# Stream 2 of a two-block transformer layer: the products of the residue groups read their moving operand in residue order

## The reference, cut to what matters

```python
ATT_GROUPS = ((128, 1), (512, 4), (2048, 16))
h = rms_norm_2(x, norm1_w)
proj = h @ w_in                      # q_b, k_b, v_b: 3 x 1536 columns of it
q_b = rms_norm_2(heads(q_b), attn_q_norm_w)
k_b = rms_norm_2(heads(k_b), attn_k_norm_w)
v_b = heads(v_b)
for gi, (window, dil) in enumerate(ATT_GROUPS):
    o_g, l_g = dilated_window_attention(q_b[:, :, gi], k_b[:, :, gi], v_b[:, :, gi],
                                        slopes[gi], dil, window // (2 * dil))
wts = jax.nn.softmax(jnp.stack(lses), axis=0)
o_b = jnp.einsum('gbsh,gbshe->bshe', wts, jnp.stack(outs))
```

## Time and profile before

| | |
|---|---|
| median of 3 runs | 3162.69 us (3160.27 to 3166.07) |
| the profiled execution's own time | 3160.64 us |
| its span in the trace | 3158.8 us |
| granted TensorE clock, mean over the span | 0.96 of 2.4 GHz |
| busy: TensorE, VectorE, ScalarE, GpSimd | 94%, 67%, 50%, 9% of the span |

### The profile page before, as it was taken

How to read it: one execution, slowest core, us unless ns; L and a number is a source line. 1 busy time by engine, 2 the same in 40 slices (tenths; PEclk the granted TensorE clock), 3 DMA queues, 4 the chain that set the end, 5 groups by cost and what they waited for, 6 DMA issues and landing times. The chain is left out here.

```text
span 3158.8 us, 46233 instructions
## 1 busy us (share of the span) xinstructions
PE 2976.5 (94%) x18534; PEld 2388.9 (76%) x18534; DVE 2114.9 (67%) x2176; ACT 1591.3 (50%) x1767; POOL 278.9 (9%) x225
## 2 busy tenths in 40 slices
PE   5999999789999999999999958997999999899999
PEld 4777787468888787788878746887778887778877
DVE  6567654569998998999899964566353344356642
ACT  3556433357777777777777733223454442333321
POOL 0110010001111111111111000442000000000000
PEclk9999999789999999999999979999999988999999
DMA  6322343369999999999999952001211122323321
GB/s 247 123 90 84 105 152 109 123 246 373 371 373 371 376 374 372 368 366 375 374 374 368 364 186 67 3 4 40 72 61 61 57 69 67 112 75 93 95 92 67
DMA packets 217372, 607.95 MB, mean 192 GB/s; under 512 B 10784, under 2 KB 118304, under 8 KB 183424
## 3 DMA queue, kind: packets, MB, share of 16 engines
q1 hardware_dynamic: 202480, 554.87, 47.6%
q0 software_dynamic: 14592, 50.36, 4.6%
q10 hardware_dynamic: 144, 0.53, 0.0%
HBM read 582.62 MB, written 23.10 MB: 192 GB/s over the span
## 5 line engine op out<-in xcount | busy, mean ns | idle before, releaser
L2475 DVE TENSOR_TENSOR weight_ring_part<-weight_ring,weight_ring_part 128x2048 fp32r<-128x2048 f32 x380 | 852.8, 2285 | 105.6 <-ACT weight_ring_part L2414 105.1
L2414 ACT ACTIVATE weight_ring_part<-weight_ring 128x2048 fp32r<-128x2048 f32 x380 | 714.3, 1915 | 257.3 <-PE ps L193 137.0
L193 PE MATMUL ps<-weight_ring_part 128*128 128x512 f32 x1456 | 584.8, 402 | 0.0
L293 DVE TENSOR_TENSOR weight_ring_part<-weight_ring,weight_ring_part 128x2048 fp32r<-128x2048 f32 x111 | 253.2, 2281 | 238.9 <-ACT weight_ring_part L290 236.4
L189 PE MATMUL ps<-weight_ring_part,gathered_hi 128*128 128x512 f32 x1024 | 409.4, 400 | 0.0
L193 PE MATMUL ps<-weight_ring_part,gathered_hi 128*128 128x512 f32 x1024 | 405.7, 396 | 0.0
L192 PE MATMUL ps<-weight_ring_part,gathered_lo 128*128 128x512 f32 x1024 | 405.6, 396 | 0.0
L189 PE MATMUL ps<-h1T_hi,weight_ring_part 128*128 128x512 f32 x872 | 363.3, 417 | 3.1 <-DVE weight_ring_part L293 1.7
L192 PE MATMUL ps<-h1T_hi,weight_ring_part 128*128 128x512 f32 x872 | 351.4, 403 | 0.0
L193 PEld LDWEIGHTS ps<-weight_ring_part 128*128 128x128 f32 x1456 | 280.2, 192 | 70.2
L290 ACT ACTIVATE weight_ring_part<-weight_ring 128x2048 fp32r<-128x2048 f32 x111 | 211.1, 1901 | 133.2 <-PE ps L193 103.9
(11 more groups left out here) (491 smaller groups left out, 4445.1 us busy)
## 6 DMA issues: line engine op xcount, KB each, us to landing
weight_ring<-in_w SPq DMA_DIRECT2D x190, 2048.0 KB, 8.7
weight_ring<-in_w_in SPq DMA_DIRECT2D x58, 1024.0 KB, 5.2
weight_ring<-in_w_ffn_up SPq DMA_DIRECT2D x44, 512.0 KB, 4.8
weight_ring<-in_w_ffn_down SPq DMA_DIRECT2D x11, 1024.0 KB, 4.8
mod_tile<-in_w_ada POOLq DMA_DIRECT2D x36, 256.0 KB, 3.0
weight_ring<-in_w_ada SPq DMA_DIRECT2D x8, 1024.0 KB, 12.8
gate_rows<-in_w_ada POOLq DMA_DIRECT2D x28, 256.0 KB, 3.2
weight_ring<-in_w_branch SPq DMA_DIRECT2D x6, 1024.0 KB, 5.5
```

Of the source, the lines that this page charges most:

```text
L193: return nc.tensor.matmul(out, x[0], y[1], start=False, stop=stop)
L293: self.nc.vector.tensor_tensor(lo, full, hi, ALU.subtract).then_inc(self.split, 1)
L2414: nc.scalar.activation(hi_half(h), full_half(h), ACT.Copy).then_inc(w_rounded, 1)
L2475: nc.vector.tensor_tensor(lo_half(h), full_half(h), hi_half(h), ALU.subtract).then_inc(w_split, 1)
```

## The change

The products of the elements of groups 1 and 2 read the moving operand with the access pattern `(j r) -> r j`, r = 4: column n of the matmul is token 4j + r, and neighbouring columns are 16 bytes apart in `h1T_hi` and `h1T_lo`. PSUM receives the element in residue order (`rows_of` gives the output the same shape, four runs of 128, which lie one behind the other). All that follows is then contiguous: the evictions of q, k and v keep the order, k's destination has no stride any more, and the squares, v and q are read in blocks of 128 (`in_blocks`) by L1203, L1194 and L1245. The output copy of the attention (L1501), which puts tokens back into natural order, stays as it was, as do group 0 and the merge.

```diff
--- before.py
+++ after.py
@@ -1178,13 +1178,19 @@
                         if k == 0 and x["kind"] == "branch":
                             pe.wait_ge(source_ready, x["source"] + 1)
                         rhs = merge["sources"][x["source"]][1:] if x["kind"] == "branch" else hT
-                        last = product(nc, ps[:, e % 2, :], cols_of(w[x["unit"]], k, P * x["part"]), [h[:, k, :] for h in rhs],
+                        last = product(nc, rows_of(x, ps[:, e % 2, :]), cols_of(w[x["unit"]], k, P * x["part"]), [in_order(x, h[:, k, :]) for h in rhs],
                                        k == 0, k == steps - 1, ring.used if k == 0 and e and elements[e - 1]["ends"] else None)
                         if k == steps - 1:
                             last.then_inc(group_ready, 1)
                             if e == len(elements) - 1:
                                 pe.wait_ge(group_ready, e + 1)
                                 nc.tensor.nop().then_inc(ring.used, 1)
+
+                    def in_order(x, row):
+                        return row.rearrange("p (j r) -> p r j", r=4) if x.get("by_residue") else row
+
+                    def rows_of(x, row):
+                        return row.rearrange("p (r j) -> p r j", r=4) if x.get("by_residue") else row
 
                     def turn_v(e):
                         x = elements[e]
@@ -1331,8 +1337,7 @@
                         if x["kind"] == "q":
                             nc.scalar.activation(x["dst"], bank, ACT.Copy).then_inc(bank_free[e % 2], 1)
                         elif x["kind"] == "k":
-                            src = bank.rearrange("p (j r) -> p j r", r=4) if x["by_residue"] else bank
-                            nc.scalar.activation(x["dst"], src, ACT.Identity, scale=x["gain"], bias=0.0).then_inc(bank_free[e % 2], 1)
+                            nc.scalar.activation(x["dst"], bank, ACT.Identity, scale=x["gain"], bias=0.0).then_inc(bank_free[e % 2], 1)
                         elif x["kind"] == "v":
                             if v_at[e] >= 2:
                                 act.wait_ge(v_turned, v_at[e] - 1)
@@ -1481,7 +1486,7 @@
                         e = batches[b]["keys"][j]
                         copied(dve, e)
                         dve.wait_ge(spread_ready, spread_at[b, j] + 1)
-                        dst = elements[e]["scaled"]
+                        dst = elements[e]["dst"]
                         nc.vector.tensor_tensor(dst, dst, ps[:, 2, :], ALU.mult).then_inc(keys_scaled, 1)
 
                     def sub_sums(h):
@@ -1709,9 +1714,9 @@
                     h = 2 * pair + part
                     row = buf[:, :, P * h:P * h + P] if kind == "v" else buf[:, h, :]
                     elements.append(dict(kind=kind, unit=3 * pair + n, part=part, ends=part, gain=gains[:, 0:1], tokens=natural,
-                                         dst=row, scaled=row, by_residue=False))
+                                         dst=row))
         batches = [dict(elements=[6 * pair + n for n in range(2, 6)], keys=[6 * pair + 4, 6 * pair + 5]) for pair in range(2)]
-        elements += [dict(kind="k", unit=6, part=g, ends=g, dst=skT[:, g, :], scaled=skT[:, g, :], by_residue=False, gain=gains[:, 1:2], tokens=natural)
+        elements += [dict(kind="k", unit=6, part=g, ends=g, dst=skT[:, g, :], gain=gains[:, 1:2], tokens=natural)
                      for g in range(2)]
         elements.append(dict(kind="v", unit=7, part=0, ends=1, dst=sv, tokens=natural))
         elements += [dict(kind="q", unit=8 + m // 2, part=m % 2, ends=m % 2, dst=sqT[:, m, :], tokens=natural) for m in range(BC)]
@@ -3322,12 +3327,11 @@
         alibi_at = arena[:, 5120:6656].rearrange("p (b h x) -> p b h x", b=2, h=2)
 
         elements, batches, units, side = [], [], [], []
+
+        def in_blocks(t):
+            return slice(P * t, P * t + P)
+
         for g in range(3):
-            step_ = 1 if g == 0 else 4
-
-            def tokens(t, step_=step_):
-                return slice(P * t, P * t + P) if step_ == 1 else slice(t, T, step_)
-
             last_unit = [None] * 4 if g == 0 else [4 * c + 3 for c in range(BC)] if g == 1 else [16 + c for c in range(BC)]
             e0 = len(elements)
             width = 3 * P if g == 0 else P
@@ -3336,10 +3340,8 @@
                     for part in range(2):
                         c = 2 * pair + part
                         row = buf[:, :, P * c:P * c + P] if kind == "v" else buf[:, c, :]
-                        by_residue = kind == "k" and g > 0
                         elements.append(dict(kind=kind, unit=6 * g + 3 * pair + n, part=part, ends=part, gain=key_gain[:, :],
-                                             dst=row.rearrange("p (r j) -> p j r", r=4) if by_residue else row, scaled=row, by_residue=by_residue,
-                                             tokens=tokens,
+                                             dst=row, by_residue=g > 0, tokens=in_blocks,
                                              scores_of=None if kind == "v" else last_unit[c], values_of=last_unit[c] if kind == "v" else None))
                 at = e0 + 6 * pair + 2
                 batches.append(dict(elements=[at + n for n in range(4)], keys=[at + 2, at + 3]))
@@ -3363,7 +3365,7 @@
                             out=[(o_g[:, 0, c, P * t:P * t + P], ps[:, 7, 0:P])]))
                 else:
                     units.append(dict(
-                        common, scores=[(512 * p + P * t, P, qT[rows[p], c, tokens(t)], kT[rows[p], c, P * t:P * t + P],
+                        common, scores=[(512 * p + P * t, P, qT[rows[p], c, P * t:P * t + P], kT[rows[p], c, P * t:P * t + P],
                                          8 * (c % 2) + 2 * t + p, here[:, p, :]) for p in range(2) for t in range(TT)],
                         seg=(8, P, P), at=32 * g + 8 * c, turns=[P * j for j in range(8)],
                         pv=[(rows[p], P * t, [(vs[p][:, t, :], 4 * p + t)]) for p in range(2) for t in range(TT)],
```

## The result

The changed kernel takes 3256.2 us in the median of 4 runs (3249.1 to 3258.8), the kernel before 3164.4 (3160.3 to 3167.9): a ratio of 1.029, 95% interval 1.0275 to 1.0308, or 87 to 97 us slower. The forecast was 3256. The profiled execution of after took 3258.8 us (span 3257.0), 98 us more than that of before.

A forecast was written before the change was run, and what follows sets the result against it. TensorE, busy 94% of the span, was taken to bound the kernel. +120 us for strided products, -26 for reads made contiguous and 0 for k's eviction gave +94 on 3162.7: 3256 us, range 3188 to 3443.

The forecast's parts named there:

- TensorE bounds stream 2, without cover: In stream 2 TensorE is always busy, so each microsecond added to it or taken away changes the kernel's time.
- Part a: 576 strided moving reads in products of groups 1 and 2: 455 ns each instead of 231, +120 us.
- The analogy: Moving reads of the products priced like strided stationary loads, whose own pace is about halved: 427 ns plus 18 and 10.
- a fixed time per line: Rival for the strided products: each line costs 1.77 ns, 854 ns per matmul, +324 us, 3486 us; chance 8%.
- a new line for every column: Strided product reads go to a new 16-byte line each column and pay; full bandwidth needs at least two hits per line.
- Part b: Strided stationary reads become contiguous: sums of squares -15.1 us, scores -10.9, transposes of v -0.2, together -26 us.
- that bound: Saving on the later reads is 0 if the clock stands at 1.2 GHz there, where contiguous loads are no faster.
- loads of 329 ns with contiguous data: Sign of being wrong, in the sums of squares: loads still at 329 ns would mean the clock has fallen.
- The stretch forecast at 337 us: Stretch with the products of groups 1 and 2, 237 us before, was to take about 337 us.
- Part c: ScalarE's eviction of k writes contiguously, 1166 to 682 ns, 8 times; hidden by TensorE's work, 0 us.
- a free stride: Rival: the stride costs the products' moving reads nothing, only -26 us is left, 3137 us; chance 10%.
- the half-hidden one: Rival: fetching ahead makes up half the loss in the products, some 330 ns each, +26 us, 3188 us; chance 10%.

The follow-up runs named there:

- moving_alone: Changed kernel with its strided moving read, but the later strided reads and strided k eviction of before put back; 3278.9 us against 3160.0 before.
- stride_two: Changed kernel with the moving read of groups 1 and 2 at 8 bytes between columns (r = 2) instead of 16; 3252.6 us.
- pairs_apart: Changed kernel with the moving read taking neighbouring pairs from each 16-byte line in two passes, and sums of squares loaded with stride two; 3247.7 us.
- stride_eight: Changed kernel with the moving read of groups 1 and 2 at 32 bytes between columns (r = 8); 3246.6 us.
- runs_swapped: Changed kernel with the moving read taking whole 16-byte lines of four columns in another order; 3139.4 us.
- natural_read: Changed kernel without its strided moving read: products, later reads and evictions all contiguous; 3126.3 us, ratio 0.9889 to the kernel before.
- evict_scatter: Changed kernel with products read contiguously and ScalarE's evictions making residue order by strided writes to SBUF; 3129.3 us, ratio 0.990 to the kernel before.
- evict_gather: Changed kernel with products read contiguously and ScalarE's evictions making residue order by strided reads of PSUM; 3128.2 us, ratio 0.9898 to the kernel before.

## Why the prediction was right, step by step

- **TensorE bounds stream 2, without cover.** Right: its busy time grew by 98.4 us and the profiled execution by 98.2.
- **Part a, 455 ns, +120 us.** Right in size: 461 ns, and 149.6 to 271.3 us is +121.7; alone (moving_alone) 112 to 123 us. That it loses little more at the lower clock was right too: 460 ns at a granted clock of 0.50, against 427 for a contiguous one. The analogy was right as a ratio, pace halved, and a fixed time per line was rightly thought unlikely.
- **The reason behind it, a new line for every column, was wrong for the moving side.** The note of the Trainium skill (SBUF — State Buffer, the note on cachelines in "Door 1: The DMA port swizzle") asks for at least two hits per line. The stationary loads agree: a stride of two takes 116 ns against 109, a stride of four 227. The moving reads don't: stride_two and pairs_apart use each line twice in a row and pay 450 ns, stride_eight pays 432, and of the patterns tried only whole lines (contiguous 231, runs_swapped some 245) keep the pace. Had the change had a stride of two, the same argument would have forecast a gain and missed by about 115 us.
- **Part b, -26 us.** The scores gave 11.7 us (10.9 forecast). The sums were mis-sized: 15.1 us forecast for the four batches of groups 1 and 2, 11.0 in the changed kernel, 13.1 in natural_read. The step took 3.49 us for each batch, which holds at the full clock (runs_swapped, with 14.0 us for the four, saved all of the 15.1); a contiguous load is nearly twice as slow at 1.2 GHz (213 against 112 ns), and the clock goes down inside most of the batches. The prediction had named that bound, 0 if the clock stands at 1.2 GHz there, and put nothing in between into the sum. It also had loads of 329 ns with contiguous data among the signs of being wrong, as they would mean a fallen clock: that sign came in part, with loads of up to 338 ns.
- **Not in the sum:** 2.5 us more in the two batches of sums of group 0, 3.9 less in the products of the merge, as fewer of them ran at 1.2 GHz, and 1.9 more in the products of group 0 and the turns. Together 121.7 - 11.0 + 2.5 - 11.7 - 3.9 + 1.9 = 99.5 us in stream 2, where the sum had 94. The stretch forecast at 337 us took 346, with the same bounds as before. That the median came out at 3256 to the microsecond is chance: the misses cancelled in part, and the medians differ by 92 us, the profiled executions by 98.
- **Part c, 0 us.** The eviction of k shrank as said (1166 to 682 ns), and evict_scatter shows its cover from the other side: 40 evictions half a microsecond longer each made no difference beside evict_gather.
- **The rivals.** For the moving read a free stride, the half-hidden one and a fixed time per line (850 ns) are excluded by 461 ns. What stays open is how a moving read is fetched: whether it wants aligned lines or just four neighbours wasn't tried.

## What to carry to other kernels

When a layout must be permuted, put the stride where the engine has slack or pays nothing: here an eviction from PSUM by ScalarE, which reads every fourth element as fast as neighbours, and not the moving operand, which is read again for each of 576 matmuls at half pace. To price an access pattern that the trace doesn't show, take the ratio from the nearest one on the same engine, but measure the pattern itself before trusting the mechanism: the ratio carried over, the rule about lines did not. And look at stationary operands with a stride of four: making them contiguous is worth some 32 us in this kernel.

## What was not expected of the hardware

- A moving read of the products (4 bytes a column) with any of the strides tried runs at about one column in 0.84 to 0.90 ns (432, 452 and 461 ns for 512 columns with strides of eight, two and four, 450 for pairs), while groups of four neighbouring columns in another order take some 245 ns against 231.
- A stationary load tells two from four: 109, 116 and 227 ns for strides of one, two and four. With a stride of four it takes 233 ns start to start at either level of the clock, a contiguous one 112 at 2.4 and 213 at 1.2 GHz.
- ScalarE reads PSUM with a stride of four in 598 ns, contiguously in 597; writing SBUF with steps of 512 bytes takes 1100.
- Products at half pace left the mean granted clock of their stretch where it was: 0.96 with them and 0.95 without (natural_read) where the small loads are contiguous, 0.93 with them (moving_alone) and 0.93 without where those are strided. That the mean rose from 0.93 to 0.96 in the changed kernel goes with the small loads.
